# A third place for expert rows from the ninth batch on, and routing's and the second tile's steps in another order

## The chip, the cores and the metric

One core of a Trainium2 chip runs the program. The metric is the device time of one execution in microseconds (us). Before the change the median of three runs is 1532.53 us (1532.36 to 1532.57).

## What is computed

Two blocks work on 256 tokens of width 1024. The first (a sparse attention, a recurrence and a convolution, two layers) isn't touched. The second computes attention over latents, an mLSTM, an output product, and then PEER, a mixture with 16384 experts, of which each token takes 16 in each of 8 heads:

```
q = (xb @ w_pq).reshape(PEER_BLOCK, PEER_HEADS, 2, PEER_DKH)
s = jnp.einsum('thpd,hpkd->thpk', q, sub_keys).astype(jnp.float32)
sv, si = lax.top_k(s, PEER_TOPK)
cand = (sv[:, :, 0, :, None] + sv[:, :, 1, None, :]).reshape(PEER_BLOCK, PEER_HEADS, -1)
best, pos = lax.top_k(cand, PEER_TOPK)
eidx = jnp.take_along_axis(cidx, pos, axis=-1)
g = jax.nn.softmax(best, axis=-1)
act = jax.nn.gelu(jnp.einsum('thkd,td->thk', expert_u[eidx], xb).astype(jnp.float32), approximate=False)
return jnp.einsum('thk,thkd->td', (g * act).astype(xb.dtype), expert_v[eidx])
```

256 tokens by 8 heads by 16 experts by one row of u and one of v (1024 floats each) are 268 MB to be gathered. All of it is in 32-bit floats.

## The kernel before

The last part of the program, from about 790 us on, is PEER. The tokens are two tiles of 128. A **turn** is one head for one tile (16 turns, listed in `TURNS`: heads 0 to 5 of tile 0, head 5 of tile 1, then both tiles of heads 6 and 7, then heads 0 to 4 of tile 1). A turn has 4 **batches** of 4 experts a token, so there are 64 batches, g = 0 to 63, and k = g // 4 is the turn.

For each batch the engines do the following, each in a fixed order that is written out by the loops over g in `peer_tensor`, `peer_vector`, `peer_scalar` and `peer_gpsimd`:

- POOL issues four indirect loads (L2871), one for each expert of a token: 128 rows of 8 KB, u beside v, into one of the 16 buffers `e_uv`. Four buffers are a **place** (`PLACE[g]`). Before it reuses a place it waits for `uv_free` of the batch that had it (`BEFORE[g]`), and for the first batch of a turn for `list_set`, the numbers of the experts.
- DVE multiplies u with the tokens and sums (L2677, `dots`), ACT takes the gelu (`e_act`), DVE multiplies with the weights (`e_w`) and spreads the result on a diagonal (`e_diag`, `diags`), and PE adds diagonal times v into PSUM (`add`), which frees the buffers. The dots write into the u half. In the first 16 batches this is done in two parts of two experts each, later in one part of four.

Between these stand the steps that choose the experts of a coming turn (`routing_at(g)`): PE multiplies tokens with `w_pq` ("queries"), ACT copies them, PE multiplies with the keys ("scores"), ACT copies them to `cond_mod_rows`, DVE takes the 16 best of each half ("halves", L2611 to L2619, `e_sv`), the 16 best sums ("candidates", `e_cand`), computes numbers and weights ("places", `e_hot`, `e_e`), PE spreads numbers and weights over partitions, DVE copies the numbers ("list", `e_listed`), ACT the weights. For turn k of 3 and more they stand at batches 4k-7 (queries), 4k-6 (scores on PE and ACT, and halves on DVE), 4k-5, 4k-4, 4k-3 (list) and 4k-2 (weights). SP loads keys and `w_pq` (1 MB) when the head changes, which is 13 times (`load_head`).

Also between them, in batches 0 to 18, stands the second tile's attention, mLSTM and output product (`second_tile_at(g)`, class `TileOnTensor` and its fellows), whose outcome is needed only for the turns of tile 1. Its data lie in the memory of places 2 and 3. So until batch 15 there are only places 0 and 1 (`ROOM_AT = 16`), and batch 16 waits for the last read of that memory, `h2T` of the second tile, which ACT ends in batch 14:

```
PLACE = [g % 2 if g < ROOM_AT else (g - ROOM_AT + 2) % 4 for g in range(BATCHES)]
...
        if BEFORE[g] is None and g >= ROOM_AT:
            pool.wait_ge(*c.taken("h2T", 1, 1))
```

In a batch each engine takes its routing and second tile steps partly ahead of its own share of the batch: PE does scores, spreads and the second tile's products before it adds; ACT copies weights and scores before the first gelu; DVE takes the maximum of the second tile's attention scores (L210) between dots and diags.

Of the kernel before, what the change touches and what calls it, by code (L numbers as in the profile page):

```python
# [14 lines left out]
P = 128  # L15
# [1446 lines left out]
def mix_memory(nc, stack, second, cond):  # L1462
# [11 lines left out]

    for name, shape in (("W", [P, 1, 2, TILES, P]), ("mixT", [P, KT, P]), ("o_gate", [P, ML_H * ML_V]),
                        ("qnT", [P, MLA_H, P]), ("hn", [P, ML_H, 2, ML_V + 1]), ("masked", [P, 1, 2, P])):
# [875 lines left out]
LEAD = 6  # L2352
# [5 lines left out]
ROOM_AT = 16  # L2358
PLACE = [g % 2 if g < ROOM_AT else (g - ROOM_AT + 2) % 4 for g in range(BATCHES)]
BEFORE = [max((f for f in range(g) if PLACE[f] == PLACE[g]), default=None) for g in range(BATCHES)]  # L2360
# [4 lines left out]
def parts_of_batch(g):  # L2365

    size = 1 if g == BATCHES - 1 else 2 if g < ROOM_AT else BATCH
    return [(c, c + size) for c in range(0, BATCH, size)]
# [6 lines left out]
def routing_at(g):  # L2375

    early = {0: [("halves", 1)], 1: [("candidates", 1), ("places", 1)], 2: [("list", 1), ("queries", 2)],
             3: [("weights", 1), ("halves", 2)], 4: [("candidates", 2)], 5: [("places", 2)], 6: [("list", 2)], 7: [("weights", 2)]}
    work = list(early.get(g, ()))
    for k in range(3, len(TURNS)):  # L2380
        for step, at_batch in (("queries", 4 * k - 7), ("halves", 4 * k - 6), ("candidates", 4 * k - 5), ("places", 4 * k - 4),
                               ("list", 4 * k - 3), ("weights", 4 * k - 2)):
            if at_batch == g:
                work.append((step, k))
    return work
# [28 lines left out]
def peer_tensor(c, m, mix, K):  # L2414
# [87 lines left out]
    def route(step, k):  # L2502
        if step == "queries":
            queries(k)
        elif step == "halves":
            scores(k)
        elif step == "list":
            list_spread(k)
        elif step == "weights":
            weights_spread(k)  # L2510
# [3 lines left out]
    def mixers(step, *a):  # L2514
# [4 lines left out]
        elif step == "levels":  # L2519
            later.levels(*a)  # L2520
            later.lstm_scores(*a)
# [29 lines left out]
    for g in range(BATCHES):  # L2551
        work = routing_at(g)
        for step in work:
            if step[0] != "queries" and step != ("halves", 1):
                route(*step)
        for step in second_tile_at(g):
            mixers(*step)
        for part in parts_of_batch(g):
            add(g, *part)
            if part[0] == 0 and 1 <= g <= MLA_H:  # L2560
                later.att_values(g - 1)
        for step in work:
            if step[0] == "queries":
                route(*step)
# [36 lines left out]
def peer_vector(c, m, mix, K, x):  # L2601
# [55 lines left out]
    def route(step, k):  # L2657
        if step == "halves":
            halves(k)
        elif step == "candidates":  # L2660
            candidates(k)
        elif step == "places":
            places(k)
# [298 lines left out]
```

## Time and profile before

| what | value |
|---|---|
| median of three runs | 1532.53 us |
| the profiled execution, own time | 1529.65 us |
| its span (first to last instruction) | 1528.3 us |
| PE / DVE / ACT / POOL busy | 1093.8 / 918.4 / 349.7 / 271.9 us |
| TensorE clock, mean share granted | 0.82 |
| bytes moved by DMA | 392.28 MB, of them 268.45 MB by POOL's indirect loads |
| first and last indirect load issued | 791.5 and 1489.6 us |
| PE, of the chain that ended last | 18% of the span; DVE 25%, DMA 8% |

The profile is of one execution, and all stretches of time below are in us from its first instruction. DMA rates say how near a stretch comes to the fastest that the trace shows. A wait is charged to the engine whose semaphore came last.

### The profile page before, as it was taken

Reading aid. Unit: us, or ns where it says so; the run is one execution under the profiler, and the core shown is the slowest. Engines: PE = TensorE matmul, PEld = TensorE weight load, DVE = VectorE, ACT = ScalarE, POOL = GpSimd, SP = SyncE. Lnnn points to the kernel's source line nnn. Section 1 sums busy time; section 2 is a strip of 40 time slices with the busy share of each in tenths; the row PEclk is TensorE's granted clock in tenths of the full one; section 3 lists DMA queues with packets and bytes.
Section 4 is the critical chain, followed back from the end, with each engine's and each line's share of the span. In section 5 each row is a group of like instructions: output and inputs, shape, how many; then the busy total and the mean of one; then the engine's idle time right before and its main releaser. Section 6 shows DMA issues by size and latency. Waiting matters only on the chain.

```text
span 1528.3 us, 17205 instructions
## 1 busy us (share of the span) xinstructions
PE 1093.8 (72%) x6243; PEld 618.8 (40%) x6243; DVE 918.4 (60%) x2429; ACT 349.7 (23%) x815; POOL 271.9 (18%) x260
## 2 busy tenths in 40 slices
PE   7997999999799849898965776656554454443534
PEld 4775655577565525543661332123111121111200
DVE  5487523348653342834446667847777778776765
ACT  2014313101431221154433442222101111111100
POOL 0000000000000000000021323344444443334340
PEclk9997999999799958998978988877656665667656
DMA  7543442454344061118039879999999999999996
GB/s 275 179 140 138 166 165 70 164 196 140 122 165 166 0 233 35 56 56 306 1 117 383 337 278 342 371 365 418 420 420 419 420 420 419 419 419 418 421 421 264
DMA packets 112662, 392.28 MB, mean 257 GB/s; under 512 B 10939, under 2 KB 40430, under 8 KB 79810
## 3 DMA queue, kind: packets, MB, share of 16 engines
q0 software_dynamic: 36864, 268.45, 42.9%
q1 hardware_dynamic: 75714, 122.74, 22.8%
q8 instruction: 49, 0.80, 0.2%
q14 instruction: 35, 0.29, 0.1%
HBM read 389.07 MB, written 1.05 MB: 255 GB/s over the span
## 4 chain that ended last, share of the span: by engine, by line
DVE 25%; PE 18%; DMA 8%; ACT 4%; issue 4%; another core or an unknown queue 3%; POOL 1%; DVEq 0%; ACTq 0%; SPq 0%
PE bank L169 17%; DVE e_uv L2677 10%; DMA e_uv<-in_experts_dram,e_listed 8%; DVE e_hot L185 1%; POOL e_uv L2871 1%; ACT L229 1%; DVE e_diag L185 1%; DVE e_rest L2615 1%; PE bank L174 1%; ACT e_h2q L229 1%; DVE e_e L210 1%; DVE e_si L2619 1%; DVE e_si L2613 1%; DVE m_W L185 1%
## 5 line engine op out<-in xcount | busy, mean ns | idle before, releaser
L2871 POOL DMA_INDIRECT e_uv<-in_experts_dram,e_listed x256 | 271.7, 1061 | 1218.4 <-DVE e_listed L202 863.2
L169 PE MATMUL bank<-e_uv,e_diag 128*32 128x512 f32 x1024 | 250.7, 943 | 314.4 <-DVE e_diag L185 301.2
L2677 DVE CUSTOM_DVE_ANT_0 e_uv<-e_uv,e_h2q 128x1024 f32<-128x1024 f32 x192 | 228.0, 1222 | 49.5 <-DMA e_uv<-in_experts_dram,e_listed 42.6
L169 PEld LDWEIGHTS bank<-e_uv,e_diag 128*32 128x32 f32 x1024 | 43.3, 147 | 469.7 <-DVE e_diag L185 360.4
L169 PE MATMUL bank<-hT,weights 128*128 128x256 f32 x640 | 150.2, 398 | 10.4 <-DVE fb L197 8.8
L169 PEld LDWEIGHTS bank<-hT,weights 128*128 128x128 f32 x640 | 127.2, 200 | 29.9 <-DVE fb L197 8.9
L169 PE MATMUL bank<-weights,hT 128*128 128x512 f32 (+1 forms) x256 | 102.3, 556 | 1.5 <-DVE hT L191 1.5
L229 ACT ACTIVATE e_act<-e_dot 128x4 f32<-128x4 f32 (+2 forms) x83 | 17.0, 204 | 353.1 <-DVE e_dot L2677 351.3
L197 DVE SCALAR_TENSOR_TENSOR conv<-ubuf,vec,conv 128x256 f32<-128x256 f32 x240 | 96.8, 480 | 0.6
L229 ACT ACT_TABLE_LOAD x73 | 93.7, 1283 | 15.3 <-PE bank L174 10.8
L169 PE MATMUL bank<-weights,mixT 128*128 128x512 f32 x192 | 91.1, 630 | 1.9 <-DVE mixT L202 1.6
L2677 DVE CUSTOM_DVE_ANT_0 e_uv<-e_uv,e_hT 128x1024 f32<-128x1024 f32 x64 | 75.8, 1219 | 8.9 <-DMA e_uv<-in_experts_dram,e_listed 8.9
L169 PEld LDWEIGHTS bank<-weights,hT 128*128 128x128 f32 x256 | 48.7, 193 | 49.0 <-issue 44.0
L169 PEld LDWEIGHTS bank<-e_hT,e_w_pq 128*128 128x128 f32 x512 | 65.6, 211 | 5.3 <-issue 5.3
L169 PE MATMUL bank<-e_hT,e_w_pq 128*128 128x128 f32 x512 | 66.6, 293 | 0.8 <-ACT e_hT L229 0.8
L169 PEld LDWEIGHTS bank<-weights,mixT 128*128 128x128 f32 x192 | 37.6, 201 | 49.6 <-issue 46.4
L185 DVE TENSOR_TENSOR x_sb<-bank,x_sb 128x512 f32<-128x512 f32 x16 | 11.1, 691 | 77.1 <-PE bank L169 77.1
L229 ACT ACTIVATE S<-S,mx 128x128 f32<-128x128 f32 (+1 forms) x64 | 29.1, 455 | 102.2 <-DVE mx L222 101.2
L2611 DVE MAX8 e_sv<-cond_mod_rows 128x8 f32<-128x128 f32 x32 | 9.4, 295 | 67.0 <-ACT cond_mod_rows L233 66.0
L169 PE MATMUL bank<-m_w,e_hT 128*128 128x464 f32 (+1 forms) x96 | 42.4, 603 | 1.9 <-DVE e_hT L192 1.9
L185 DVE TENSOR_TENSOR e_w<-e_act,e_weight 128x4 f32<-128x4 f32 (+2 forms) x83 | 13.5, 162 | 48.5 <-ACT e_act L229 41.6
L222 DVE CUSTOM_DVE_ANT_0 S<-bank,constants 128x128 f32<-128x128 f32 (+1 forms) x64 | 22.9, 358 | 21.7 <-PE bank L169 16.7
(375 smaller groups left out, 1458.3 us busy)
## 6 DMA issues: line engine op xcount, KB each, us to landing
weights<-in_w_in_dram SPq DMA_DIRECT2D x16, 2048.0 KB, 7.7
weights<-in_w_ada_dram SPq DMA_DIRECT2D x8, 2048.0 KB, 8.1
e_w_pq<-in_w_pq_dram SPq DMA_DIRECT2D x13, 1024.0 KB
weights<-in_w_out_dram SPq DMA_DIRECT2D x6, 2048.0 KB, 7.7
weights<-in_cmp_w_dram SPq DMA_DIRECT2D x4, 2048.0 KB, 7.9
m_w<-in_w_in_dram SPq DMA_DIRECT2D x2, 2048.0 KB, 11.4
m_wo<-in_w_ada_dram SPq DMA_DIRECT2D x2, 2048.0 KB
m_w<-in_w_ada_dram SPq DMA_DIRECT2D x2, 2048.0 KB, 9.9
```

The lines of the kernel that those rows point to most:

```text
L169: ins = self.engine.matmul(out, lhsT, rhs, start=start, stop=stop, **kw)
L174: ins = self.engine.transpose(out, a, ident)
L185: return self.mark(self.engine.tensor_tensor(out, a, b, op), tell)
L197: return self.mark(self.engine.scalar_tensor_tensor(out, a, s, b, op0, op1), tell)
L210: return self.mark(self.engine.tensor_reduce(out, a, AX.X, op), tell)
L222: return self.mark(self.engine.tensor_tensor_reduce(out, a, b, scale, init, op0, op1, total), tell)
L229: return self.mark(self.engine.activation(out, a, func, **kw), tell)
L2613: dve.mark(c.nc.vector.max_index(out_i[:, 0:8], out_v[:, 0:8], values))
L2615: dve.mark(c.nc.vector.match_replace(scratch, out_v[:, 0:8], values, -3e38))
L2619: return dve.mark(c.nc.vector.max_index(out_i[:, 8:16], out_v[:, 8:16], scratch))
L2677: dve.mark(c.nc.vector.tensor_tensor_reduce(u, u, h2q[tt][n], 1.0, 0.0, MUL, ADD, m["dot"][:, j:j + 1]), ("dots_set", g, c0) if n == c1 - ...
L2871: ins = c.nc.gpsimd.indirect_dma_start(out=m["uv"][j], out_offset=None, in_=A["experts"], in_offset=bass.IndirectOffsetOnAxis(ap=of, axis=0))
```

## The change

The second tile's keys and values, `knT`, `krT`, `qrT`, its queries `qnT`, `vm`, `lkT`, `lqT` and `M`, now lie together exactly under place 2. They are last read by the attention's values in batch 4 (`att_values`) and the mLSTM's scores in batch 6. So place 2 is open from batch 8, place 3 from batch 17, and each batch takes the place that was used longest ago. Five heads lead instead of six, so one head less is loaded twice (12 loads of `w_pq`). Routing's steps are split finer and put at other batches, some "late" (.5), which is behind the batch's last part on DVE. On PE scores, spreads and weights now come behind the batch's first add, on ACT behind the gelus, and ACT copies queries behind the next batch's first gelu. On DVE the maximum of the attention scores comes behind the first diags.

```diff
-            ("wo", [P, 4096]), ("gt1", [P, D]), ("v_ext", [P, TILES, ML_H, ML_V + 1]), ("knT", [P, MLA_H, 2 * T]),
-            ("krT", [P, 2, 2 * T]), ("qrT", [P, 2, T]), ("vm", [P, TILES, MLA_H, MLA_V]), ("lkT", [P, 2, 2 * T]),
-            ("lqT", [P, 2, T]), ("M", [ROWS2, 2 * T]), ("qk_lat", [P, 4, T + 2]), ("k_ctx", [P, 2, T + 2]),
+            ("knT", [P, MLA_H, 2 * T]), ("krT", [P, 2, 2 * T]), ("qrT", [P, 2, T]), ("qnT", [P, MLA_H, P]),
+            ("vm", [P, TILES, MLA_H, MLA_V]), ("lkT", [P, 2, 2 * T]), ("lqT", [P, 2, T]), ("M", [ROWS2, 2 * T])):
...
-LEAD = 6
+LEAD = 5
...
-ROOM_AT = 16
+ROOM_AT = {2: 8, 3: 17}
+def places_of_batches():
+    place, before, latest = [], [], {0: None, 1: None}
+    for g in range(BATCHES):
+        latest.update({p: None for p, first in ROOM_AT.items() if first == g})
+        p = min(latest, key=lambda p: (-1 if latest[p] is None else latest[p], p))
+        place.append(p)
+        before.append(latest[p])
+        latest[p] = g
+    return place, before
...
+ROUTING_STEPS = ("queries", "scores", "halves", "candidates", "places", "spread", "list", "weights")
+ROUTING_AT = {1: (None, None, 0, 1, 1.5, 2, 2.5, 3), 2: (2, 3, 4, 4.5, 5, 6, 6.5, 7), 3: (5, 6, 7, 8, 8.5, 9, 9.5, 10),
+              5: (14, 15, 15.5, 16, 16.5, 17, 17.5, 18)}
+for turn in (4, *range(6, len(TURNS))):
+    start = 4 * turn - 8
+    ROUTING_AT[turn] = (*range(start, start + 6), start + 5.5 if start + 5 < ROOM_AT[3] else start + 6, start + 6)
...
 def second_tile_at(g):
-    work = [("att_scores", g)] if g < MLA_H else []
-    work += [("att_turned", g - 1)] if 1 <= g <= MLA_H else []
-    work += [("outputs", g - 5)] if 5 <= g < 5 + ML_H else []
-    work += [("levels", g - 4)] if 4 <= g < 4 + ML_H else []
+    work = [("att_turned", g - 1)] if 1 <= g <= MLA_H else []
+    work += [("att_scores", g)] if g < MLA_H else []
+    work += [("levels", g - 3)] if 3 <= g < 3 + ML_H else []
+    work += [("outputs", g - 4)] if 4 <= g < 4 + ML_H else []
+    work += [("lstm_scores", g - 3)] if 3 <= g < 3 + ML_H else []
...
     for g in range(BATCHES):
-        work = routing_at(g)
-        for step in work:
-            if step[0] != "queries" and step != ("halves", 1):
-                route(*step)
         for step in second_tile_at(g):
             mixers(*step)
         for part in parts_of_batch(g):
             add(g, *part)
+            if part[0] == 0:
+                if 1 <= g <= MLA_H:
+                    later.att_values(g - 1)
+                route(routing_at(g), "scores", "spread", "weights")
+        route(routing_at(g), "queries")
...
+            if BEFORE[g] is None and PLACE[g] == 2 and n == 0:
+                pool.wait_ge(*at("att_values", 1, MLA_H - 1))
+            if BEFORE[g] is None and PLACE[g] == 2 and n == BATCH - 1:
+                pool.wait_ge(*c.full("lstm_scores", 1, ML_H - 1))
+            if BEFORE[g] is None and PLACE[g] == 3 and n == 0:
+                pool.wait_ge(*c.taken("h2T", 1, 1))
```

What this does to the order is shown at two places. First PE, at the choice of turn 3 of the program, before; the rows with `e_hT` are its queries, with `e_keysT` its scores, with `e_uv` the adds:

```order
L169 MATMUL bank<-e_uv,e_diag 32x512 x8
L174 MATMUL bank<-constants,e_keys 128x128 x2
L169 MATMUL bank<-e_hT,e_w_pq 128x128 x16
L169 MATMUL bank<-e_e,constants 32x4 x16
L169 MATMUL bank<-e_keysT,e_qT 128x128 x2
L169 MATMUL bank<-m_v_ext,m_W 128x129 x7
L169 MATMUL bank<-m_M,constants 128x128 x2
L169 MATMUL bank<-m_lqT,m_lkT 128x128 x4
L174 MATMUL bank<-constants,m_k_ctx 128x128 x4
L169 MATMUL bank<-e_uv,e_diag 32x512 x8
```

And the same place now:

```order
L169 MATMUL bank<-e_uv,e_diag 32x512 x8
L174 MATMUL bank<-constants,e_keys 128x128 x2
L169 MATMUL bank<-e_hT,e_w_pq 128x128 x16
L169 MATMUL bank<-m_M,constants 128x128 x2
L169 MATMUL bank<-m_v_ext,m_W 128x129 x7
L169 MATMUL bank<-m_lqT,m_lkT 128x128 x4
L174 MATMUL bank<-constants,m_k_ctx 128x128 x4
L169 MATMUL bank<-e_uv,e_diag 32x512 x4
L169 MATMUL bank<-e_e,constants 32x4 x16
L169 MATMUL bank<-e_keysT,e_qT 128x128 x2
L169 MATMUL bank<-e_uv,e_diag 32x512 x4
```

The scores, which stood right behind the queries and ahead of the next add, are now a batch's first half behind that add.

Second DVE, in the regular turns past batch 20 (before: `e_listed` is turn k's list, the rows L2611 to L2619 on `e_sv` and `e_si` are the next turn's halves), before (a pair of `ISA` rows is one dot product; where a line of "..." stands are the batch's other dot products):

```order
L2677 ISA e_uv,e_dot<-e_uv,e_h2q 128x1024
L2677 ISA e_dot 128x1
L202 CAST e_listed<-bank 128x16
L185 TENSOR_TENSOR e_w<-e_act,e_weight 128x4
L185 TENSOR_TENSOR e_diag<-constants,e_w 128x128
...
L2677 ISA e_uv,e_dot<-e_uv,e_h2q 128x1024
L2677 ISA e_dot 128x1
L2611 MAX e_sv<-cond_mod_rows 128x8
L2613 MAX_INDEX e_si<-e_sv,cond_mod_rows 128x8
```

And now (the functions stand some lines further down in the file):

```order
L185 TENSOR_TENSOR e_w<-e_act,e_weight 128x4
L185 TENSOR_TENSOR e_diag<-constants,e_w 128x128
...
L2696 ISA e_uv,e_dot<-e_uv,e_h2q 128x1024
L2696 ISA e_dot 128x1
L202 CAST e_listed<-bank 128x16
L2629 MAX e_sv<-cond_mod_rows 128x8
```

The list has moved one batch later, from batch 4k-3 to 4k-2, and stands directly ahead of the next turn's halves, which have kept their place behind the dots of batch 4k-2 while their scores are made a batch earlier.

## Rows read from the trace of the kernel before

**Rows 1.** The page, slices: GB/s moved in 40 equal slices of 38.2 us.
```profile
GB/s 275 179 140 138 166 165 70 164 196 140 122 165 166 0 233 35 56 56 306 1 117 383 337 278 342 371 365 418 420 420 419 420 420 419 419 419 418 421 421 264
```

**Rows 2.** Windows by stage; the header names the columns.
```profile
core 0: us, PE busy (x) PEld busy (x) DVE busy (x) ACT busy (x) POOL busy (x), PEclk, DMA share, GB/s
791.50:830.00 38.50, 20.73 (x120) 10.56 (x122) 23.69 (x69) 11.37 (x22) 13.79 (x14) 0.81 0.96 387
830.00:884.00 54.00, 37.49 (x244) 18.10 (x240) 35.03 (x97) 23.06 (x47) 15.39 (x16) 0.91 0.88 329
884.00:930.00 46.00, 35.75 (x236) 19.01 (x236) 30.24 (x91) 18.31 (x40) 10.83 (x11) 0.90 0.79 283
930.00:1011.00 81.00, 50.56 (x328) 21.17 (x328) 58.78 (x164) 21.12 (x51) 27.09 (x26) 0.84 0.91 354
1011.00:1100.00 89.00, 52.28 (x578) 25.25 (x578) 60.77 (x160) 15.49 (x37) 41.09 (x39) 0.71 1.01 415
1100.00:1480.00 380.00, 178.50 (x1468) 70.11 (x1468) 283.79 (x729) 44.83 (x112) 159.02 (x148) 0.63 1.02 420
```

**Rows 3.** Timeline of POOL: start, us, engine, line, operation [idle before, releaser].
```profile
890.07 0.94 POOL L2871 DMA_INDIRECT e_uv<-in_experts_dram,e_listed  x1 [0.30 <-issue]
...
900.59 0.94 POOL L2871 DMA_INDIRECT e_uv<-in_experts_dram,e_listed  x1 [9.58 <-PE bank L169]
...
907.72 0.94 POOL L2871 DMA_INDIRECT e_uv<-in_experts_dram,e_listed  x1 [4.58 <-PE bank L169]
...
916.85 0.94 POOL L2871 DMA_INDIRECT e_uv<-in_experts_dram,e_listed  x1 [6.95 <-PE bank L169]
...
1008.56 1.55 POOL L2871 DMA_INDIRECT e_uv<-in_experts_dram,e_listed  x1 [9.27 <-DVE e_sif L202]
```

**Rows 4.** Timeline of PE, turn 3 of routing.
```profile
888.96 4.15 PE L169 MATMUL bank<-e_hT,e_w_pq 128*128 128x128 f32 x32
...
893.57 0.71 PE L169 MATMUL bank<-e_keysT,e_qT 128*128 128x128 f32 x4
```

**Rows 5.** Timeline of ACT, the same stretch.
```profile
894.32 0.37 ACT L233 COPY cond_mod_rows<-bank 128x256 f32<-128x256 f32 x1 [0.80 <-PE bank L169]
894.81 0.20 ACT L229 ACTIVATE e_act<-e_dot 128x2 f32<-128x2 f32 x1
```

**Rows 6.** Timeline of DVE, two of the waits for a gelu.
```profile
895.04 0.16 DVE L185 TENSOR_TENSOR e_w<-e_act,e_weight 128x2 f32<-128x2 f32 x1 [6.54 <-ACT e_act L229]
...
1003.78 0.16 DVE L185 TENSOR_TENSOR e_w<-e_act,e_weight 128x2 f32<-128x2 f32 x1 [7.15 <-ACT e_act L229]
```

**Rows 7.** Waits of DVE, 797 to 884 us: total, times, longest.
```profile
DVE m_small L210 <- PE bank L169: 16.0, 4, 6.8
```

**Rows 8.** Waits of DVE, 884 to 1016 us.
```profile
DVE e_w L185 <- ACT e_act L229: 26.0, 17, 7.2
```

**Rows 9.** Waits, 1060 to 1500 us.
```profile
POOL e_uv L2871 <- DVE e_listed L202: 63.7, 10, 9.7
...
DVE e_sv L2611 <- ACT cond_mod_rows L233: 52.1, 9, 8.8
```

**Rows 10.** Timeline: first load, first dot product.
```profile
791.54 1.07 POOL L2871 DMA_INDIRECT e_uv<-in_experts_dram,e_listed  x1 [791.09 <-DVE e_listed L202]
...
797.33 1.23 DVE L2677 CUSTOM_DVE_ANT_0 e_uv<-e_uv,e_hT 128x1024 f32<-128x1024 f32 x1 [6.07 <-DMA e_uv<-in_experts_dram,e_listed]
```

**Rows 11.** Tile e_uv on POOL, from 1055.7 us: the one load issued at 1055.74.
```profile
DMA to landing us min/median/max: 21.1/21.1/21.1
```

**Rows 12.** Timeline of DVE: that load's dot product, and a later one.
```profile
1082.52 1.22 DVE L2677 CUSTOM_DVE_ANT_0 e_uv<-e_uv,e_h2q 128x1024 f32<-128x1024 f32 x1
...
1083.85 0.17 DVE L202 CAST e_listed<-bank 128x16 uint32<-128x16 f32 x1
...
1374.30 1.23 DVE L2677 CUSTOM_DVE_ANT_0 e_uv<-e_uv,e_h2q 128x1024 f32<-128x1024 f32 x1 [0.76 <-DMA e_uv<-in_experts_dram,e_listed]
```

**Rows 13.** The page, DMA issues.
```profile
e_w_pq<-in_w_pq_dram SPq DMA_DIRECT2D x13, 1024.0 KB
```

More of the change, by code:

```diff
@@ L2500, in add, with route @@
                       tell=(f"uv_free{PLACE[g]}{n // 2}", g) if h and n % 2 else None)
[L2502 to L2510, printed above, removed]
+    def route(steps, *names):
+        for step, k in steps:
+            if step not in names:
+                continue
+            if step == "queries":
+                queries(k)
+            elif step == "scores":
+                scores(k)
+            elif step == "spread":
+                list_spread(k)
+            elif step == "weights":
+                weights_spread(k)
     first, later = TileOnTensor(c, mix, K, 0), TileOnTensor(c, mix, K, 1)
@@ L2520, in mixers @@
             later.levels(*a)
+        elif step == "lstm_scores":
             later.lstm_scores(*a)
@@ L2655, in listed, with route @@
         dve.copy(m["listed"][:, k % 2], bank_k[:, 2 * P + BUFS:2 * P + 2 * BUFS], tell=("list_set", k))
[L2657 to L2663, printed above, removed]
-        elif step == "list":
-            listed(k)
+    def route(steps):
+        for step, k in steps:
+            if step == "halves":
+                halves(k)
+            elif step == "candidates":
+                candidates(k)
+            elif step == "places":
+                places(k)
+            elif step == "list":
+                listed(k)
     def dots(g, c0, c1):
@@ L2703, in mixers @@
     def mixers(step, *a):
-        if step == "att_scores":
-            later.att_max(*a)
-        elif step == "att_out":
+        if step == "att_out":
             later.attention_out()
@@ L2718, in mixers_after @@
     def mixers_after(step, *a):
-        if step == "levels":
+        if step == "att_scores":
+            later.att_max(*a)
+        elif step == "levels":
             later.masked(*a)
@@ L2727, in peer_vector @@
     first.filled(m["hT"], 1)
-    for step in ("halves", "candidates", "places", "list"):
-        route(step, 0)
+    halves(0)
+    candidates(0)
+    places(0)
+    listed(0)
     for g in range(BATCHES):
-        parts = parts_of_batch(g)
-        dots(g, *parts[0])
+        one, *others = parts_of_batch(g)
+        dots(g, *one)
         for step in second_tile_at(g):
             mixers(*step)
-        if g >= ROOM_AT:
-            for step in routing_at(g):
-                route(*step)
-        diags(g, *parts[0])
+        if not others:
+            route(routing_at(g))
+        diags(g, *one)
         for step in second_tile_at(g):
             mixers_after(*step)
-        if g < ROOM_AT:
-            for step in routing_at(g):
-                route(*step)
-        for more in parts[1:]:
+        if others:
+            route(routing_at(g))
+        for more in others:
             dots(g, *more)
             diags(g, *more)
+        route(routing_at(g, late=True))
         if g == (LAST_OF[0] + 1) * PER_TURN:
@@ L2797, in quarter_set, with route @@
                      tell=c.banks.emptied("h2q", tt, q, half))
+    def route(steps, *names):
+        for step, k in steps:
+            if step not in names:
+                continue
+            if step == "queries":
+                queries(k)
+            elif step == "scores":
+                scores(k)
+            elif step == "candidates":
+                soft(k)
+            elif step == "weights":
+                weighted(k)
     first, later = TileOnScalar(c, mix, K, x, 0), TileOnScalar(c, mix, K, x, 1)
```

62 lines of the change are left out of this document (22 added, 40 removed).

## The prediction, made before the changed kernel was run

> **What bounds the kernel now.** I read the page's slices first. Past slice 27 the rate stays at 418 to 422 GB/s until the end [rows 1]: there the gathering of expert rows fills the DMA engines and sets the end. From slice 22 to 27 it is 278 to 383. So the question is how much of the 268 MB has been moved before the rate settles, and the windows by stage answer it [rows 2]. The long one, 1100 to 1480 us, gives 420 GB/s at a DMA share of 1.02; I take 420 as full. A stretch of length L at rate r has then lost L x (1 - r/420):
>
> - 791.5 to 830: 38.5 x (1 - 387/420) = 3.0 us
> - 830 to 884: 54 x (1 - 329/420) = 11.7 us
> - 884 to 930: 46 x (1 - 283/420) = 15.0 us
> - 930 to 1011: 81 x (1 - 354/420) = 12.7 us
> - 1011 to 1100: 89 x (1 - 415/420) = 1.1 us
>
> Together 43.5 us. Since everything behind is bound by the DMA, a microsecond won back here comes out at the end, and one lost there too.
>
> Why the rate falls shows in POOL's timeline. It has loads to issue and waits for buffers: between 890.07 and 900.59 nothing is issued, then pairs of loads at 900.59, 907.72 and 916.85 [rows 3]. With eight buffers only two batches can be under way. And the wait that holds a batch there is one of order, not of work. PE makes the queries of turn 3 from 888.96 on and the scores at 893.57 [rows 4]; ACT must copy the scores at 894.32 before it may take a gelu at 894.81 whose input had long been there [rows 5]; DVE sits idle 6.54 us for that gelu, and 7.15 us at the same place two turns later [rows 6]. DVE's waits for gelus are 26.0 us in 17 times from 884 to 1016 [rows 8]. Before 884 the counterpart is L210, the maximum of the attention scores, for which DVE waits 16.0 us in 4 times ahead of its diags [rows 7]. The last hole is POOL's wait until 1008.56, where batch 16 asks for the second tile's memory [rows 3].
>
> **The change, part by part.**
>
> *Place 2 from batch 8, and the gelu ahead of the scores' copy* (one term, as each makes room for the other). DVE is busy 30.2 us of the 46 and 58.8 of the 81 between 884 and 1011 [rows 2], 89 of 127. Of its 38 idle us the four long gelu waits are about 22 (26.0 less 13 short ones of 0.3 us [rows 8]); with the scores behind a first add and their copy behind the gelu they go. DVE then needs 127 - 22 = 105 us for the stretch, and the DMA 127 - 15.0 - 12.7 = 99. So DVE's bound leaves at most 22, the DMA's 28. In this stretch the third place makes it possible that POOL issues batch 9 with batch 8 and doesn't wait for another batch to be freed. Batch 8 itself comes hardly earlier: its list stands at the end of DVE's batch 6, about where the old load at 907.72 stood. What is late next is DVE: its work per batch comes near the 10 us that four loads of 1.05 MB take at 420 GB/s. I take 19 of the 22: something is left where PE (busy 86 of the 127 [rows 2]) stands in the way. Ends: 8 (the first window's half alone) and 27.7 (all of both windows). Place 3's wait for `h2T`, now at batch 17, is inside this: with three places in use it has a batch more to come.
>
> *The attention's maximum behind the first diags, the finer routing in batches 0 to 7.* At most 11.7 + 3.0 us are to be had there [rows 2]. DVE's 16.0 us of L210 waits [rows 7] don't vanish whole: PE still makes the attention scores ahead of its adds, and the 0.8 us of maximum lie in another place. Below, 0; above, 14.7; I take 6, half of what the 830 to 884 window has lost, since two places remain two places.
>
> *One head less loaded.* 12 loads of `w_pq` instead of 13 [rows 13], 1.05 MB, with 0.13 MB of keys: 1.18 MB / 420 GB/s = 2.8 us. It falls in the full stretch, where nothing hides it, so it counts whole. PE's key transposes and copies that go with it are beside the DMA and cost nothing while that is the bound.
>
> *The list one batch later from turn 6 on.* This takes something away. POOL already waits 63.7 us in ten times for lists there [rows 9]; now it may issue a turn's first batch only when DVE is through the dots of batch 4k-2, and then only the four loads of batch 4k-1 are still on their way: 10 us of DMA work instead of 20. A load issued into idle DMA engines is landed within 797.33 - 791.54 = 5.8 us [rows 10]. So the cover holds if DVE is not later than about 10 - 5.8 = 4.2 us behind the landing. How late is it? The load issued at 1055.74 landed 21.1 us later, at 1076.8 [rows 11], and its dot product began at 1082.52 [rows 12]: 5.7 us. Around 1374.30 the dot product begins on the landing, 0 us [rows 12]. The lateness comes from the halves step, for which DVE waits 52.1 us in nine turns [rows 9], 5.8 a turn; with scores a batch ahead this wait goes, and batch 4k-3 now holds no routing on DVE at all. So I expect DVE to come up with the DMA within a few turns and the list to cost nothing then, and 3 us in the first two or three turns together. Ends: 0, and 10 turns x (5.7 - 4.2) = 15 us.
>
> *Small ones, at nothing.* The new wait for `att_values` and `lstm_scores` at batch 8: both are done in batches 4 and 6. The load of `w_pq` for turn 6 has two batches instead of four to land, about 20 us; the trace has no landing of such a load, so it may hold PE for up to some 5 us once, and then landed batches in the three or four places keep the DMA going; if they didn't, 5 us are lost. ACT has one table load more, beside other work.
>
> **A rule weighed.** The windows show 354 GB/s from 930 to 1011 and 420 later, on the same kind of loads [rows 2], so 354 is no ceiling and the gap can be won. The Trainium skill, "DMA: Bandwidth & Descriptors", section "Specifications", states an HBM limit for one core of about 358 GB/s; by that the last window of the stretch would already be full and the 12.7 us not to be had. The trace disagrees for 380 us on end, and the page itself says below that a core whose neighbour is idle gets more.
>
> **The sum.** -19 - 6 - 2.8 + 3 = -24.8 us. On the profiled span: 1528.3 - 24.8 = 1503.5. The profiled execution's own time of 1529.65 lies 2.9 under the median; I keep that difference and take the sum off the median: 1532.5 - 24.8 = 1507.7 us. What this measurement can tell from no change is 0.2%, 3 us.
>
> **The rivals.**
>
> 1. *The order in PE and ACT keeps holding the batches.* The third place fills with landed rows that nobody takes, since DVE and PE stand in the same in-order queues and the two bind in turn. Then of the 884 to 1011 stretch only half of the first window comes back, 8, nothing of the early one, and 2.8 less 3 for head and list: about -8, 1524.7. For: DVE, PE and DMA are each within 30% of full there. Against: the 6.54 and 7.15 us waits [rows 6] are exactly at rows that the change moves.
> 2. *Everything comes back.* The DMA stays full from the first load on but for its start: 43.5 - 2 + 2.8, some -44: 1488.5. Against: DVE's bound of 105 us for the stretch, where the DMA would need 99.
> 3. *The late list starves the DMA in each turn* (slower). If DVE stays late, POOL gets its list when the rows in flight run out. The price of a turn is DVE's lateness less 4.2 us, ten times. The early gains of 27.8 us are eaten from a lateness of 4.2 + 2.8 = 7 us on, in all turns; at 8.5 us it is 43 - 27.8 = +15, 1547.7. For: three full places at batch 17 may make DVE 10 us late, and it was 5.7 late in rows 11 and 12. Against: without the halves' wait DVE gains some 6 us a turn on what it did, so that lateness can't last ten turns.
> 4. *Place 2 isn't really open*, since the list of batch 8 comes at the end of batch 6. It bounds batch 8 alone; batches 9 to 11 have their list. I count it in rival 1.
>
> **How the numbers follow.** Forecast 0.72, rival 1 0.14, rival 2 0.08, rival 3 0.06. The forecast's own range, inside the ends of its terms: 10 + 2 + 2.8 - 3 = 12 less at the weak end, 24 + 10 + 2.8 - 0 = 37 at the strong one, 1496 to 1521. To hold the time 8 times in 10 it has to reach rival 1 and some way towards rival 2: 1493 to 1526. Faster by over 0.2%: the forecast, rival 2 and rival 1 but for 0.03, so 0.91; within: that 0.03; slower: rival 3, 0.06.
>
> **What would show it.** In the changed profile: POOL issues eight loads in a row where batch 8 begins, at about 890 to 907; the windows up to there reach about 350 GB/s and from there on over 400, and 420 starts some 100 us earlier than at 1011; no DVE wait of over 3 us for a gelu past 884; no wait of DVE for scores in the regular turns; POOL's waits for lists grow from 6.4 to over 10 us each, with the rate still at 418 to 421. I would be wrong if the rate dips in each regular turn (rival 3), if POOL's waits for PE between 890 and 1000 stay (rival 1), or if DVE's busy share there goes to over 0.95 (rival 2).

## The result and the profile after

The changed kernel took 1514.82 us (median of 4 runs, 1513.20 to 1515.22), the kernel before beside it 1532.44 us. The ratio is 0.989, with a 95% interval of 0.9871 to 0.9909: 17.6 us faster, where 24.8 were forecast. 1514.82 lies inside the forecast's range of 1496 to 1521. The span of the profiled execution is 1513.8 us against 1528.3.

The windows of the changed kernel by stage, with the columns of [rows 2]:

```profile
791.50:830.00 38.50, 25.32 (x88) 11.22 (x90) 20.62 (x60) 11.37 (x22) 13.05 (x13) 0.72 1.01 403
830.00:884.00 54.00, 40.44 (x272) 22.63 (x268) 39.87 (x110) 28.51 (x57) 18.81 (x16) 0.90 0.79 304
884.00:930.00 46.00, 35.88 (x218) 17.25 (x218) 30.90 (x90) 14.35 (x33) 17.69 (x17) 0.88 0.82 317
930.00:1011.00 81.00, 57.87 (x451) 25.50 (x450) 61.12 (x168) 22.33 (x54) 35.56 (x34) 0.84 1.01 420
1011.00:1100.00 89.00, 46.48 (x479) 22.49 (x478) 72.29 (x194) 17.41 (x40) 35.10 (x31) 0.69 0.98 401
1100.00:1465.00 365.00, 157.93 (x1436) 68.66 (x1436) 269.76 (x687) 41.17 (x104) 149.75 (x137) 0.65 1.01 418
```

and what lies behind 1465 us, before and now:

```profile
1465.00:1528.30 63.30, 25.20 (x103) 4.56 (x97) 34.73 (x68) 2.01 (x10) 13.10 (x14) 0.61 0.79 327
1465.00:1513.80 48.80, 21.67 (x80) 4.21 (x80) 26.95 (x54) 1.80 (x9) 9.83 (x10) 0.64 0.75 314
```

With the prediction's own measure, length x (1 - rate / 420), the losses are now 1.6, 14.9, 11.3, 0, 4.0 and 1.7 us, together 33.5 where it was 43.5. That is 10.0 us. The bytes of the head's load that is gone are 2.8. By the same measure the end behind 1465 us loses 12.3 us where it lost 14.0, which is 1.7 less. The sum, 14.5, is the difference of the two spans. The first expert load is also issued earlier, at 789.75 instead of 791.54, but that is no further term: in neither run do the DMA engines move anything from 789 to 791.5 us, so whatever it gives is already in the first window (403 against 387). (The median of the runs of before lies 2.8 us above its profiled execution, that of the changed kernel 0.4 below its own, hence 17.6 and not 14.4.)

Window by window: 930 to 1011 gave back all of its 12.7 us, 884 to 930 only 3.7 of 15.0. The stretch before 884 lost 1.8 more than it did, and two new losses stand behind 1011, of 2.9 and 1.7 us.

**The first hole, 898 to 906.** Windows of 8 us around the two holes:

```profile
898.00:906.00 8.00, 7.04 (x54) 3.19 (x56) 2.29 (x6) 3.87 (x9) 1.46 (x1) 0.57 0.18 66
...
1034.00:1042.00 8.00, 4.95 (x132) 3.34 (x124) 5.36 (x12) 1.97 (x6) 4.44 (x3) 0.98 0.63 226
```

66 GB/s is 6.7 us lost, 226 is 3.7. POOL's timeline at the first, to hold against [rows 3]:

```profile
889.90 0.94 POOL L2903 DMA_INDIRECT e_uv<-in_experts_dram,e_listed  x1 [0.30 <-issue]
904.54 1.67 POOL L2903 DMA_INDIRECT e_uv<-in_experts_dram,e_listed  x1 [13.71 <-DVE e_listed L202]
906.52 0.93 POOL L2903 DMA_INDIRECT e_uv<-in_experts_dram,e_listed  x1 [0.30 <-issue]
```

Batch 8 has its place (for three of its loads) but not its list: 13.71 us of waiting with nothing issued. In the kernel before, the first load of batch 8 is the one at 900.59 of [rows 3]; so it now comes 4 us later than it did. Then nine loads follow with no wait over 0.6 us. DVE shows why the list is late:

```profile
902.54 0.16 DVE L185 TENSOR_TENSOR e_w<-e_act,e_weight 128x2 f32<-128x2 f32 x1 [6.84 <-ACT e_act L229]
904.10 0.17 DVE L202 CAST e_listed<-bank 128x16 uint32<-128x16 f32 x1 [1.14 <-PE bank L169]
```

The list (`e_listed`) stands behind batch 6's last gelu, and that gelu behind the second tile's mLSTM on ACT:

```profile
894.78 1.28 ACT L229 ACT_TABLE_LOAD   x1 [2.06 <-PE bank L169]
896.08 0.83 ACT L229 ACTIVATE m_W<-m_masked,m_gcol 128x128 f32<-128x128 f32 x2
896.95 1.96 ACT L229 ACTIVATE m_W<-bank,m_gcol 128x128 f32<-128x128 f32 x5
898.94 0.38 ACT L233 COPY m_hn<-bank 128x258 f32<-128x258 f32 x1
900.12 0.58 ACT L233 COPY m_mixT<-bank 128x512 f32<-128x512 f32 x1 [0.80 <-PE bank L174]
900.72 1.28 ACT L229 ACT_TABLE_LOAD   x1
```

So the wait of 6.54 us of [rows 6] is not gone. It is as long as it was, with another cause: no longer the copy of routing's scores, now seven activations for `m_W`, two copies and two table loads (`ACT_TABLE_LOAD`) of 1.28 us each.

**The second hole, 1034 to 1042**, in POOL's timeline, then PE's and DVE's:

```profile
1036.95 1.67 POOL L2903 DMA_INDIRECT e_uv<-in_experts_dram,e_listed  x1 [25.14 <-DVE e_listed L202]
```

```profile
1027.05 5.47 PE L169 MATMUL bank<-e_hT,e_w_pq 128*128 128x128 f32 x32 [2.12 <-DMA e_w_pq<-in_w_pq_dram]
```

```profile
1036.51 0.17 DVE L202 CAST e_listed<-bank 128x16 uint32<-128x16 f32 x1 [5.90 <-PE bank L169]
```

PE takes up the queries of turn 6, waits for their weights, multiplies 5.47 us, and only then comes to batch 17's adds and, behind them, to the spread of turn 5's numbers. DVE waits 5.90 us for it, and POOL with DVE.

**Waits over stretches.** From 797 to 884, from 884 to 1016 and from 1060 to 1480 us (total, times, longest), for [rows 7], [rows 8] and [rows 9]:

```profile
DVE m_small L210 <- PE bank L169: 10.5, 3, 5.1
DVE e_w L185 <- ACT e_act L229: 9.8, 9, 3.8
POOL e_uv L2903 <- DVE e_listed L202: 6.2, 1, 6.2
```

```profile
POOL e_uv L2903 <- PE bank L169: 34.6, 10, 8.3
POOL e_uv L2903 <- DVE e_listed L202: 25.9, 3, 13.7
DVE e_w L185 <- ACT e_act L229: 21.0, 16, 7.6
```

```profile
POOL e_uv L2903 <- DVE e_listed L202: 158.7, 10, 19.0
DVE e_uv L2696 <- DMA e_uv<-in_experts_dram,e_listed: 54.0, 51, 2.6
...
DVE e_sv L2629 <- ACT cond_mod_rows L233: 0.8, 1, 0.8
```

DVE's waits for scores in the regular turns are gone (52.1 to 0.8 us), POOL's for lists have grown from 63.7 to 158.7 us in ten times, and the rate stayed at 418 all the same. The gelu waits past 884 went from 26.0 only to 21.0. POOL's waits for PE from 884 to 1016, a sign that the prediction named for rival 1, more than halved, to 34.6 us from this in the kernel before:

```profile
POOL e_uv L2871 <- PE bank L169: 76.1, 16, 9.6
```

These totals also move without any change: in a second profile of the kernel before (run 12) DVE's gelu waits past 884 are 21.5 us, its waits for scores in the regular turns 4.3 us and POOL's for lists 87.6 us, with the same 420 GB/s there.

### The profile page after: what moved, and what is told of

The parts are those of the page before. It is cut to its first block, busy times and chain, and to the rows that moved or that the text cites. A ratio compares the mean times of both kernels' runs of the same rounds, so it can differ in the third digit from the quotient of the medians.

```text
span 1513.8 us, 17204 instructions
## 1 busy us (share of the span) xinstructions
PE 1083.6 (72%) x6241; PEld 624.0 (41%) x6241; DVE 920.6 (61%) x2431; ACT 350.8 (23%) x816; POOL 281.4 (19%) x260
## 4 chain that ended last, share of the span: by engine, by line
DMA 19%; PE 15%; DVE 13%; POOL 8%; ACT 4%; issue 4%; another core or an unknown queue 1%; DVEq 0%; ACTq 0%; SPq 0%
DMA e_uv<-in_experts_dram,e_listed 17%; PE bank L169 14%; POOL e_uv L2903 8%; DVE e_uv L2696 4%; DMA e_w_pq<-in_w_pq_dram 2%; ACT L229 1%; PE bank L174 1%; ACT e_h2q L229 1%; ACT m_W L229 1%; DVE m_W L185 1%; DVE e_hT L192 1%; DVE e_hot L185 0%; DMA e_h2q<-in_final_g_dram 0%; DVE e_diag L185 0%
## 5 line engine op out<-in xcount | busy, mean ns | idle before, releaser
L2903 POOL DMA_INDIRECT e_uv<-in_experts_dram,e_listed x256 | 281.2, 1099 | 1196.9 <-DVE e_listed L202 1005.3
L169 PE MATMUL bank<-e_uv,e_diag 128*32 128x512 f32 x1024 | 240.9, 899 | 313.5 <-DVE e_diag L185 294.8
L2696 DVE CUSTOM_DVE_ANT_0 e_uv<-e_uv,e_hT 128x1024 f32<-128x1024 f32 x64 | 76.0, 1219 | 12.7 <-DMA e_uv<-in_experts_dram,e_listed 12.7
L169 PEld LDWEIGHTS bank<-e_hT,e_w_pq 128*128 128x128 f32 x512 | 69.5, 222 | 10.1 <-issue 7.8
L169 PE MATMUL bank<-e_hT,e_w_pq 128*128 128x128 f32 x512 | 70.8, 305 | 3.0 <-DMA e_w_pq<-in_w_pq_dram 2.1
L185 DVE TENSOR_TENSOR x_sb<-bank,x_sb 128x512 f32<-128x512 f32 x16 | 11.1, 691 | 74.5 <-PE bank L169 74.5
```

The lines of the kernel that those rows point to most:

```text
L169: ins = self.engine.matmul(out, lhsT, rhs, start=start, stop=stop, **kw)
L185: return self.mark(self.engine.tensor_tensor(out, a, b, op), tell)
L2696: dve.mark(c.nc.vector.tensor_tensor_reduce(u, u, h2q[tt][n], 1.0, 0.0, MUL, ADD, m["dot"][:, j:j + 1]), ("dots_set", g, c0) if n == c1 - ...
L2903: ins = c.nc.gpsimd.indirect_dma_start(out=m["uv"][j], out_offset=None, in_=A["experts"], in_offset=bass.IndirectOffsetOnAxis(ap=of, axis=0))
```

## The experiments

With the first chip called A, they ran on three others: runs 1, 2, 4 and 5 on B, runs 3, 6, 7 and 8 on C, and runs 9 to 12 on D. The kernel before took 1523.45, 1522.90 and 1522.51 us there, not 1532.44. So kernels are compared by their ratio to the runs of before beside them, or within a group. Expectations in microseconds that were written for chip A have to be read as ratios too.

**1 and 2. Each half alone.** The order without the place:

```
-ROOM_AT = {2: 8, 3: 17}
+ROOM_AT = {2: 17, 3: 17}
```

> The changed kernel with place 2 opened at batch 17 as place 3 is, so only the order of steps, the five leading heads and the memory layout are left of the change. Theory room (the third place closes the holes between 930 and 1011 us, the order alone only shortens DVE's waits): the holes come back, about 10 of the 12.7 us; time 1522 to 1527. Theory order (the holes closed because the gelu no longer stands behind the scores' copy): the time stays within 3 us of the changed kernel's 1514.8.

Measured: 1516.07 us (1515.24 to 1516.65), ratio 0.9949 (0.9932 to 0.9965). And the place without the order: the kernel before with the memory laid out anew, `places_of_batches()` and `ROOM_AT = {2: 8, 3: 17}`, with the old `ROUTING_AT`, the old order in each batch and six heads ahead.

> The kernel before with nothing but the third place from batch 8 (the memory layout and the planner of places), its order of steps and six leading heads kept. Theory room: the holes between 930 and 1011 close for the most part, and since the list of batch 8 stands earlier in this order (batch 6, behind the first part), batch 8 is issued at about 897; time 1511 to 1519. Theory order: DVE's waits of 6 to 7 us for gelus stay and hold the batches as before; time 1526 to 1532.

Measured: 1515.39 us (1512.48 to 1516.10), ratio 0.9941 (0.9924 to 0.9958). Windows from 830 to 1011, first of the order alone:

```profile
830.00:884.00 54.00, 39.39 (x272) 22.49 (x269) 39.56 (x110) 28.85 (x58) 19.18 (x16) 0.91 0.85 320
884.00:930.00 46.00, 36.94 (x218) 17.38 (x218) 31.29 (x91) 14.01 (x31) 13.07 (x12) 0.83 0.81 304
930.00:1011.00 81.00, 56.92 (x472) 25.23 (x470) 63.35 (x171) 22.33 (x54) 38.10 (x34) 0.84 0.99 394
```

and of the place alone, with its waits of DVE for gelus from 884 to 1016 us:

```profile
830.00:884.00 54.00, 38.07 (x248) 18.10 (x240) 35.02 (x97) 23.07 (x47) 15.39 (x16) 0.91 0.86 325
884.00:930.00 46.00, 35.68 (x236) 19.01 (x236) 31.21 (x92) 18.32 (x40) 14.58 (x15) 0.89 0.83 312
930.00:1011.00 81.00, 53.46 (x380) 22.40 (x384) 62.28 (x173) 21.34 (x52) 31.03 (x29) 0.81 1.02 416
```

```profile
DVE e_w L185 <- ACT e_act L229: 20.8, 17, 6.5
```

and the same waits with the order alone:

```profile
DVE e_w L185 <- ACT e_act L229: 10.6, 15, 6.8
```

What follows:

- (a) Each half gives 7 to 8 us on this chip. Run 1 has five heads ahead, so by the bytes 2.8 us of its 7.4 are the head's load. The halves don't add up: together they would be 15.4 us, and the whole change gave 10.2 us in run 3, with a ratio whose interval overlaps both of theirs. One reason is the second hole: from 1011 to 1100 each half alone has 419 and 418 GB/s, the two together 402 (run 3).
- (b) The place alone brings 930 to 1011 to 416 GB/s while DVE still waits 20.8 us for gelus from 884 to 1016. The third place doesn't shorten these waits. So moving the gelu ahead of the scores is not what the full rate hung on. The order alone does shorten them, to 10.6 us, and gets 394 GB/s.
- (c) Before 884, where both have two places, the new order gives 320 GB/s and the old 325: it wins nothing there.
- (d) The place alone leaves 884 to 930 at 312 GB/s. Batch 8 is issued from 898.08 on, but its fourth load waits until 911.71, 10.21 us, for PE; in the old order the mLSTM's last scores, which that load has to wait for, stand at batch 7 and not at 6.

As ratios the expectation "room" for run 1 was 0.9932 to 0.9965, and 0.9949 came; for run 2 it was 0.986 to 0.991, and 0.9941 came, so the place alone brought less than "room" had it, and more than "order" (0.9958 to 0.9997).

**3. The changed kernel again**, on chip C, as the base of its group.

> The changed kernel itself, on the chip of the following runs, as their measure: the kernel before took 1532.4 us beside it the first time, and 1523.5 beside the four experiments so far, so times of different chips can't be set against each other. If the ratio of 0.989 belongs to the kernels, it comes again within 0.003; if the gain was partly a matter of that chip, it comes nearer to 1.

Measured: 1512.75 us (1510.01 to 1515.15), ratio 0.9932 (0.9912 to 0.9952), 10.2 us under the kernel before. The interval lies outside that of the first comparison, and the ratio did not come again within 0.003: part of the 17.6 us belongs to chip A. The changed kernel differs by 2.1 us between the two chips, the kernel before by 9.5; run 12 looks at that.

**4, 5 and 6. The lists of turns 2 and 5 earlier**, each alone and both. Spread and list come one batch earlier: turn 2's from batch 6 to 5, turn 5's from 17 to 16, so ahead of the last gelu of batch 6 and of the queries of turn 6. Turn 5's candidates and numbers move half a batch with it. Both edits:

```
-ROUTING_AT = {..., 2: (2, 3, 4, 4.5, 5, 6, 6.5, 7), ...
-              5: (14, 15, 15.5, 16, 16.5, 17, 17.5, 18)}
+ROUTING_AT = {..., 2: (2, 3, 4, 4.5, 5, 5, 5.5, 7), ...
+              5: (14, 15, 15.5, 15.5, 16, 16, 16.5, 18)}
```

> The changed kernel with turn 2's spread at batch 5 and its list at the end of batch 5 instead of 6. Theory list (between 896 and 905 us the DMA ran empty because POOL waited 13.7 us for this list with place 2 open): POOL issues batch 8 right behind batch 7, at about 891 to 893, the hole of about 8 us closes, and 6 to 9 us come out: 1506 to 1509. Theory processing (the first seven batches are limited by PE, ACT and DVE in turn, and loads that land sooner only wait longer): within 2 us of 1514.8.

> The changed kernel with turn 5's candidates at the end of batch 15, numbers and spread at 16 and list at the end of batch 16 instead of 17. Theory list (between 1034 and 1041 us the DMA ran nearly empty, POOL had waited 25 us for this list): the list comes some 12 us earlier, the dip to about 0.6 of the rate goes, 3 us come out: 1511 to 1513. Theory processing: within 1 us of 1514.8, because PE, held by the late w_pq of turn 6 and its queries, frees the places no sooner.

> The changed kernel with both lists early, turn 2's at the end of batch 5 and turn 5's at the end of batch 16. Theory list (each of the two holes is its own loss of DMA time, and what is won in the first isn't lost in the second): 9 to 12 us less than the changed kernel on the same chip, no window under 400 GB/s past 890 us. Theory debt (rows that land sooner are only held longer, DVE and PE set the pace up to batch 20): at most 6 us less, as the better of the two alone.

Measured: turn 2's list 1507.57 us (1506.46 to 1509.61), ratio 0.9892 (0.9876 to 0.9909); turn 5's list 1510.35 us (1509.25 to 1510.99), 0.9912 (0.9895 to 0.9928); both 1503.23 us (1501.52 to 1503.97), 0.9866 (0.9849 to 0.9882), 9.5 us under the changed kernel beside it. With both, POOL at the first and the last load of batch 8:

```profile
889.43 0.93 POOL L2903 DMA_INDIRECT e_uv<-in_experts_dram,e_listed  x1 [0.30 <-issue]
...
894.36 0.94 POOL L2903 DMA_INDIRECT e_uv<-in_experts_dram,e_listed  x1 [0.72 <-PE bank L169]
```

DVE's wait for the gelu:

```profile
900.83 0.16 DVE L185 TENSOR_TENSOR e_w<-e_act,e_weight 128x2 f32<-128x2 f32 x1 [6.84 <-ACT e_act L229]
```

And the windows:

```profile
884.00:930.00 46.00, 38.00 (x194) 18.28 (x191) 32.55 (x94) 14.02 (x31) 17.98 (x18) 0.83 1.00 407
930.00:1011.00 81.00, 53.73 (x468) 24.19 (x468) 65.44 (x184) 26.70 (x62) 36.03 (x33) 0.86 0.99 402
1011.00:1100.00 89.00, 52.12 (x555) 25.37 (x552) 74.68 (x191) 13.99 (x36) 37.80 (x32) 0.70 1.02 420
```

This settles the first hole. The gelu wait of 6.84 us is the same, to the hundredth, and the rate is 407 in place of 319: with its list ahead of that wait the whole window loses 1.4 us. What held the stream was the place of the list behind that gelu. By windows the changed kernel on the same chip lost 11.1 (319), 0 (420) and 3.8 us (402) in the three, this one 1.4, 3.5 and 0: 10.0 us less. With the other windows and the end it is 8.4 less, and the two profiled spans differ by 8.2 us (1510.8 and 1502.6), the medians by 9.5. By their ratios the single edits are worth 6.1 and 3.0 us against the changed kernel on the other chip, so they nearly add up; with turn 2's list alone the second hole grew (389 GB/s from 1011 to 1100, a loss of 6.6 us), and turn 5's list closed it.

**7. The regular lists earlier** (turns 6 on, one batch, where they stood before the change), nothing else.

```
+    if turn >= 6:
+        ROUTING_AT[turn] = (*range(start, start + 5), start + 4, start + 5, start + 6)
```

> The changed kernel with the list of turns 6 to 15 where it stood before the change, in batch 4k-3, with the spread a batch earlier for it. Theory cover (four loads on their way are enough, the late list costs nothing in the regular turns): within 2 us of the changed kernel on the same chip, the rate from 1100 to 1465 us goes from 418 to 420 at most, POOL's waits for lists fall from 15 us each to about 6. Theory starved (the DMA runs short in each turn): 5 to 15 us less.

Measured: 1510.70 us (1509.01 to 1512.34), ratio 0.9917 (0.9900 to 0.9933), 2.0 us under the changed kernel, with intervals that overlap. The windows from 1100 to 1465 read 420 against 419, 0.9 us. So the late list costs 0 to 2 us in all: the term "3, between 0 and 15" was near the truth.

**8. The regular lists one batch later still**, to have rival 3's mechanism in the open: `(*range(start, start + 6), start + 7, start + 6)`.

> The changed kernel with the list of turns 6 to 15 one batch later still, 4k-1: the suspected cost doubled. Then no load is on its way when POOL gets the list. Theory cover: each of ten turns has a hole of 1.2 us for the last dot product, 0.6 for list and issue and 2 to 3 until data flow, 4 to 5 us together, 40 to 50 us more in all. If instead POOL and DVE had slack beyond the four loads, the time would stay within 5 us.

Measured: 1565.73 us (1563.58 to 1566.96), ratio 1.0275 (1.0258 to 1.0292): 53 us more for ten turns. The window from 1011 to 1100 has 377 GB/s; the last one, and a load of POOL's:

```profile
1100.00:1465.00 365.00, 142.57 (x1276) 61.14 (x1276) 246.21 (x629) 37.10 (x94) 124.72 (x117) 0.64 0.91 371
```

```profile
1225.90 1.00 POOL L2905 DMA_INDIRECT e_uv<-in_experts_dram,e_listed  x1 [24.54 <-DVE e_listed L202]
```

The expectation was 40 to 50 us. POOL waits 24.54 us here, in the changed kernel up to 19.8 on this chip at 419 GB/s. The first is starvation, the second is not: the length of the wait doesn't tell, the rate beside it does. Rival 3's mechanism is real, and shows one batch behind where the change stops.

**9. Six heads ahead again in the changed kernel** (`LEAD = 6`), for the price of the head's load.

> The changed kernel with six head loads in each queue instead of five. Theory (the load given up is bytes that the stream has to carry nowhere else): 1.18 MB more at some 420 GB/s, 2.8 us above the changed kernel, so 1515 to 1516 us where the changed kernel gives 1512.7. Rival (the head's load only fills DMA time that the stages before the experts leave free, or a later start of the first list): within 1 us of the changed kernel.

Measured: 1513.51 us (1512.49 to 1515.86), ratio 0.9939 (0.9922 to 0.9957), against 0.9932 for the changed kernel on another chip; spans 1511.1 and 1510.8. By the time alone this looks like the rival, a load that costs nothing. The windows suggest otherwise. With six heads 1011 to 1100 gives 420 where the changed kernel gives 402:

```profile
1011.00:1100.00 89.00, 44.79 (x473) 21.00 (x470) 74.08 (x194) 15.48 (x37) 38.44 (x32) 0.71 1.02 420
```

since turn 6 then belongs to the head of turn 5 and PE needs no new `w_pq` there. In the changed kernel on chip C the load of `w_pq` (issue list from 990 to 1050 us, last number: us to landing), and PE:

```profile
e_w_pq<-in_w_pq_dram SPq DMA_DIRECT2D x1, 1024.0 KB, 26.2
```

```profile
1025.55 5.79 PE L169 MATMUL bank<-e_hT,e_w_pq 128*128 128x128 f32 x32 [4.35 <-DMA e_w_pq<-in_w_pq_dram]
```

So the 2.8 us saved by one head less were spent again at turn 6, 3.8 us by the window, as long as turn 5's list stands behind the queries: with that list earlier the same window has 420 GB/s with five heads too (runs 5 and 6). The other windows don't all agree: with six heads the first one has 409 GB/s instead of 393, 1.5 us less lost, with the first load issued 1.4 us earlier, and 416 instead of 419 from 1100 to 1465 takes 2.6 back, for a reason that stays open. The comparison is across two chips, and its interval of 2.6 us to either side is as wide as the price itself: the windows suggest the reading, the time doesn't prove it.

**10 and 11. Both lists, and turn 6's queries a batch later; then the regular lists too.**

```
+    if turn == 6:
+        ROUTING_AT[turn] = (17, 18, 19, 20, 21, 21, 22, 22)
+    if turn >= 7:
+        ROUTING_AT[turn] = (*range(start, start + 5), start + 4, start + 5, start + 6)
```

> The changed kernel with the lists of turns 2 and 5 earlier, as in the run of both lists (1503.2 us beside a kernel before of 1522.9, ratio 0.9866), and turn 6's steps spread so that its w_pq has a third batch before PE multiplies by it. Theory (PE waited for w_pq, and its queue held adds that the stream was waiting for): PE's wait for w_pq of 2.1 us is gone, and the window of 1011 to 1100 us stays at 420 GB/s or gains up to 1.5%, 0.5 to 2 us in all, a ratio of 0.9855. Rival (with the list early, nothing waits for those adds any longer): ratio 0.9866, within 0.001.

> As the run before, and in each turn from the seventh on the list one batch earlier, before the last quarter of the projections. Theory (the late list of the regular turns costs about 2 us in all, as the run with those lists alone showed, 1510.7 beside 1512.7): 1 to 2 us under the run before it, ratio 0.985, and POOL's waits for lists after 1060 us halved. Rival (POOL waits without DMA running dry, so the list's place costs nothing): the same time as the run before it, within 1 us.

Measured: without the last two lines 1502.95 us (1501.96 to 1503.99), ratio 0.9865 (0.9848 to 0.9881); with them 1501.93 us (1500.67 to 1503.45), 0.9859 (0.9843 to 0.9876). The first is the ratio of run 6 to 0.0001: with the list ahead, PE's wait for `w_pq` holds nothing, as its rival said. The last is the fastest of all, 20.6 us under the kernel before on its chip. Its 1.0 us over the run beside it is within the spread; its windows from 1100 to 1465 read 420 against 417, POOL's waits for lists after 1060 went from 178.5 to 93.4 us.

**12. The kernel before again**, on chip D.

> The kernel before, unchanged, with a profile on this chip. It took 1532.4 us on the first chip and 1523 on two others. Theory (the lost time between chips lies where the stream starves: 884 to 930 and 930 to 1011 us, since how late a list or a gelu comes depends on small differences of ACT and PE): the two windows read 5 to 10% more GB/s than the 283 and 354 of the first profile, and the regular turns the same 420. Rival (another chip's memory or DMA is faster throughout): the regular turns read 422 to 424 GB/s in place of 420, and the span shrinks evenly.

Measured: 1523.80 us (1521.05 to 1525.70), span 1522.4 against 1528.3 in the first profile.

```profile
791.50:830.00 38.50, 23.27 (x90) 11.19 (x92) 24.55 (x71) 11.23 (x22) 13.19 (x14) 0.77 0.99 399
830.00:884.00 54.00, 36.69 (x242) 17.92 (x238) 34.72 (x99) 23.27 (x48) 15.39 (x16) 0.91 0.86 322
884.00:930.00 46.00, 35.69 (x236) 19.02 (x236) 31.11 (x93) 18.11 (x39) 11.59 (x12) 0.91 0.78 289
930.00:1011.00 81.00, 54.53 (x406) 23.25 (x408) 62.43 (x173) 22.23 (x54) 31.06 (x29) 0.81 0.96 372
1011.00:1100.00 89.00, 46.85 (x536) 21.27 (x532) 69.18 (x176) 17.68 (x41) 41.48 (x39) 0.72 1.01 420
```

```profile
1002.92 1.54 POOL L2871 DMA_INDIRECT e_uv<-in_experts_dram,e_listed  x1 [8.19 <-DVE e_sif L202]
```

The full rate is 420 on both. Of the 5.9 us between the spans 3.5 lie in 930 to 1011 (354 to 372), 1.1 in the window behind it, 0.9 ahead of it and 0.5 behind 1465. The expectation of 5 to 10% more in the two windows was met in the second alone (5%; 283 to 289 is 2%). Batch 16's first load, 1008.56 in [rows 3], comes at 1002.92. A likely reading is that small differences in the order of arrival are paid for where the DMA starves, and hidden where there is a place more. That fits the changed kernel's smaller spread between chips. What differs between the chips at the root stays open, and one profile of each is thin.

## Why the prediction was right or wrong

**What bounds the kernel: right.** Every run comes to 418 to 420 GB/s in its best window, and the spans follow the lost microseconds, the end behind 1465 included: 14.5 of 14.5 here (with the head's 2.8), 8.4 of 8.2 between runs 3 and 6, 5.9 of 5.9 in run 12.

**Place 2 and the gelu ahead of the scores: right in size, half wrong in mechanism.** 19 was forecast, 3.7 + 12.7 = 16.4 came on chip A. On chips D and C (one profile of each kernel, runs 12 and 3) the kernel before lost only 23.6 us in the two windows (289 and 372 GB/s), the changed one 11.1: 12.5. The prediction took the gelu waits away and got DVE's new bound from it. They stayed, 21.0 us of 26.0, one of 7.6 at 1006.49, and "no DVE wait of over 3 us for a gelu past 884" is plainly refuted. The step that failed is that the new order makes them go: it does shorten them where there are two places (10.6 us in run 1), but hardly with three (21.0, and 17.4 in run 3). I had followed the one cause that the trace showed at that place, and not what comes to stand there when it is moved: the mLSTM's seven activations on the same engine. That the rate rose all the same is the third place's work for the most part (run 2). The 24 at the strong end of the range was also more than the 22 that the prediction's own bound for DVE left.

**Batch 8 and its list: the step that failed.** The prediction says that batch 8 "comes hardly earlier", as its list stands at the end of batch 6, counts it in rival 1, and among its signs still lists eight loads in a row from about 890. They came at 904.54. The comparison with "the old load at 907.72" was a misreading: that is the third load of the old batch 8, whose first is the one at 900.59 [rows 3]. In the window from 884 to 930 it cost 9.7 us (11.1 less 1.4, runs 3 and 6), of which run 6 gives 3.5 back behind it. So rival 4 was the largest mechanism left, and had no price of its own. It could have had one from the prediction's own figures: with a first load at about 907.72 nothing is issued for nearly 18 us from 890 on, and the four loads of batch 7, at most, are then still on their way, 10 us at the full rate.

**The early stretch: wrong.** 6 us won were forecast, 1.8 were lost. Order against order on one chip, 0.7 were lost (320 and 325 GB/s from 830 to 884). DVE's wait for the attention's maximum did shrink, 16.0 to 10.5 us, but the waits for gelus grew there from 2.7 to 9.8 us, and 6.2 us of POOL's for a list appeared. With two places, what one step no longer holds the next one does. The prediction's own lower end, "two places remain two places", was the better argument.

**One head load less: right as bytes, wrong as a sum.** 12 loads instead of 13, 1.18 MB; but the wait for `w_pq` at turn 6, "at nothing", was covered by nothing. The guess of up to 5 us for PE was right (2.1 and 4.4 us); the mistake was the cover. It named landed batches, while what stood behind the waiting PE was the spread of turn 5's list, and POOL waited 25.14 us for that list. Run 3 measured the load of `w_pq`, issued by SP at 999.26 into a stream that ran at 417 GB/s from 999 to 1026, at 26.2 us to landing. The Trainium skill, "DMA: Bandwidth & Descriptors", section "Anatomy of one DMA — SWDGE (gpsimd) path", fits about 2.0 us plus bytes over 436 GB/s to one transfer issued by POOL, by which an estimate for this size is 4.4 us. No run here shows such a load by itself, so the 26.2 us neither bear that fit out nor refute it.

**The late list of the regular turns: right.** 3 forecast, 0.9 to 2.0 by run 7, with the rate unbroken, DVE's waits for scores gone and POOL's for lists grown as foretold. One part of the argument isn't borne out: DVE was to catch up with the DMA because 52.1 us of waits for scores go. In the kernel before on chip D these waits are 4.3 us, and DVE already waits for landing rows, 94.8 us in 87 times (1060 to 1500). The second hole, at turn 5's list, belongs to this family and took 2.9 more. Rival 3's point of decision lies between this order and one batch later (run 8).

**The sum.** -16.4 + 1.8 - 2.8 + 2.9 + 1.7 - 1.7 (the end behind 1465, which I had not foreseen) = -14.5 on the span. That the time came out inside the range owes something to chip A, where the kernel before had the most to lose: on chip C 10.2 us were gained, less than the 12 of the forecast's weak end. Rival 1 (-8) comes near there, but not by its reason.

## What to carry over

In a stream that is fed from queues in order, ask of each load which item it waits for last, its buffer or its list of addresses, and move the list ahead of every wait in that engine's queue that is not its own: here that was worth 9.5 us for two lists, more than either half of the change alone (7.4 and 8.1). A buffer more didn't shorten the waits here (20.8 us with it, 21.5 without); the rate rose beside them, so count the lost rate and not the waits. And a step moved out of an engine's way leaves a gap for what stood behind it: read what that is before the whole wait is booked as won.

## What the runs showed of the hardware

- A load of 1 MB in SP's queue took 26.2 us to land beside POOL's row loads in run 3, and 26.1 in run 9, with all loads together at 417 GB/s meanwhile in both: 40 GB/s for it. The prediction had left it about 20.
- The Trainium skill, "DMA: Bandwidth & Descriptors", section "Specifications", puts the HBM limit of a core at about 358 GB/s, and the page adds further down that a core whose neighbour is idle gets more. For this core by itself 358 was no limit: the window from 930 to 1011 us, at 354 before, gives 420 in the changed kernel, and every run has a window of 418 or more.
- The same kernel took 1532.4 us on one chip and 1522.5 to 1523.8 on three others, with runs of one chip within about 5 us. In one profile from each of two chips the full DMA rate was the same, 420 GB/s, and the difference lay for the most part where the stream starves.
